# A long two-block network on one core: the experts' second chunk of weights waits in SBUF and is copied into place, and the out-projection of the recurrence begins inside its last pair

## What is computed

```python
def moe_swiglu(xn, w_router, w_gate, w_up, w_down):
    ...
    for e in range(N_EXPERTS):
        y = y + combine[:, e:e + 1] * swiglu(xt, w_gate[e], w_up[e], w_down[e])

def rwkv7_mixer(h, ...):
    ...
    for d in range(2):
        ...
        o = rwkv7_scan(*ins)
        ...
        dir_out.append((group_norm(o, gn_w, gn_b) + bonus.reshape(nB, S, D)) * g.astype(F32))
    y = dir_out[0] + dir_out[1]
    return y.astype(h.dtype) @ w_o
```

## Time and profile before

| what | value |
|---|---|
| three runs | 2826.64, 2830.97, 2832.77 us |
| the profiled execution's own time | 2826.99 us |
| its span | 2825.3 us |
| PE busy | 2639.8 us (93%) |
| DVE, ACT, POOL busy | 672.7, 431.5, 87.9 us |
| HBM read | 568.37 MB, mean 203 GB/s |

### The profile page before, as it was taken

One profiled execution on the slowest core, in us unless ns is written; L12 is line 12 of the kernel. 1 busy time (PEld: TensorE's weight loads), 2 busy tenths in 40 slices (PEclk: granted clock), 3 DMA queues, 4 the chain that ended last, 5 costly groups with the idle time before them and its releaser, 6 DMA issues. The chain is left out here.

```text
span 2825.3 us, 76095 instructions
## 1 busy us (share of the span) xinstructions
PE 2639.8 (93%) x34633; PEld 2195.9 (78%) x34633; DVE 672.7 (24%) x1740; ACT 431.5 (15%) x1040; POOL 87.9 (3%) x168
## 2 busy tenths in 40 slices
PE   8899999989979999999999999899999799989998
PEld 6677777668869999989989897666667688877664
DVE  4511000181120110110110101410043577761001
ACT  1111000111110100100100101410011444441000
POOL 0100000010000000000000000000000000010000
PEclk9899999999989999999999999999999898889999
DMA  7344344543429999999999995354443000002442
GB/s 216 119 136 135 120 157 139 154 133 119 152 79 399 407 407 407 408 407 407 407 407 407 407 400 172 112 174 155 156 142 119 5 7 5 6 5 97 158 153 89
DMA packets 290525, 571.23 MB, mean 202 GB/s; under 512 B 18326, under 2 KB 181140, under 8 KB 290404
## 3 DMA queue, kind: packets, MB, share of 16 engines
q1 hardware_dynamic: 290404, 569.49, 55.8%
HBM read 568.37 MB, written 5.28 MB: 203 GB/s over the span
## 5 line engine op out<-in xcount | busy, mean ns | idle before, releaser
L1793 PE MATMUL ps<-xg,ring 128*64 128x80 f32 x14336 | 516.4, 234 | 7.7 <-issue 2.3
L1793 PEld LDWEIGHTS ps<-xg,ring 128*64 128x64 f32 x14336 | 503.5, 138 | 18.6 <-DMA ring<-in_moe_w_up_dram 9.3
L1388 PE MATMUL ps<-xT,ring 128*128 128x256 f32 x1728 | 379.8, 380 | 4.7 <-PEq L452 3.0
L1388 PEld LDWEIGHTS ps<-xT,ring 128*128 128x128 f32 x1728 | 328.8, 190 | 65.2 <-issue 22.4
L1400 PE MATMUL ps<-ring,hidden 128*128 128x512 f32 x688 | 301.8, 593 | 0.0
L1809 PE MATMUL ps<-hidden,expert_down 128*64 128x80 f32 x7168 | 260.3, 233 | 10.4 <-DVE hidden L1885 5.7
L1809 PEld LDWEIGHTS ps<-hidden,expert_down 128*64 128x64 f32 x7168 | 252.0, 137 | 16.8 <-DVE hidden L1885 7.6
L1400 PEld LDWEIGHTS ps<-ring,hidden 128*128 128x128 f32 x688 | 131.0, 190 | 147.2 <-issue 145.1
L618 PE MATMUL ps<-ring,xT 128*128 128x256 f32 (+1 forms) x1056 | 225.8, 376 | 7.2 <-PEq L1269 3.9
L618 PEld LDWEIGHTS ps<-ring,xT 128*128 128x128 f32 x1056 | 197.0, 194 | 34.6 <-issue 9.0
L618 PE MATMUL ps<-xT,ring 128*128 128x256 f32 (+1 forms) x944 | 213.3, 388 | 11.1 <-PEq L596 4.5
(11 more groups left out here) (384 smaller groups left out, 2474.7 us busy)
## 6 DMA issues: line engine op xcount, KB each, us to landing
ring<-in_moe_w_gate_dram SPq DMA_DIRECT2D x128, 896.0 KB, 16.6
ring<-in_moe_w_up_dram SPq DMA_DIRECT2D x128, 896.0 KB, 16.8
expert_down<-in_moe_w_down_dram SPq DMA_DIRECT2D x96, 1024.0 KB, 17.3
ring<-in_mlp_w_dram SPq DMA_DIRECT2D x64, 1024.0 KB, 5.4
ring<-in_w_xkv_dram SPq DMA_DIRECT2D x16, 1024.0 KB, 5.3
expert_down<-in_moe_w_down_dram SPq DMA_DIRECT2D x32, 512.0 KB, 16.5
ring<-in_ffn_w_gate_dram SPq DMA_DIRECT2D x11, 1024.0 KB, 5.5
ring<-in_ffn_w_up_dram SPq DMA_DIRECT2D x11, 1024.0 KB, 5.3
```

The source lines that it names most:

```text
L1388: mm = pe.matmul(bank[:, m * SEQ:(m + 1) * SEQ], w[:, c, m * P:(m + 1) * P], self.xT[:, c, :], start=(c == 0), stop=(c == KC - 1))
L1793: mm = pe.matmul(bank[b][o:o + HEAD, at, :], w[:, c, f * P + o:f * P + o + HEAD], xg[:, p * E_STEP + c, :], start=(p == 0 and c == 0 and a ...
```

## The change

1. **A waiting place.** A tile `second` of 56 KB per partition lives through the first block: 8 pieces of 1792 elements. The tiles named under "Places in SBUF" become parts of it, and so cost no room of their own. `expert_waiting(kind, p, n)` gives the place of a gate or up piece.
2. **The second chunk is loaded ahead.** `expert_ahead_gate` also loads both halves of chunk 1's gate weights and the first half of its up weights (a half is two pieces in one transfer, 1792 KB); `expert_ahead_up` also loads the second half of the up weights.
3. **Eleven chunks are moved into place.** For chunks 1 to 11 (`MOVED = 11`, the items 0 to 2 less the first chunk) the gate and up weights land in `second`, and are copied into their slot in `ring` when PE is done with the piece there: gate pieces by ACT, up pieces by POOL. Such a copy waits for the half's transfer and for the piece's last product, and only then may PE read the piece. SP loads the next chunk but one into the waiting place: the order becomes gate and up of chunk g + 1, then down of chunk g. ACT's and SP's loops over the first 3 items are written out; from item 3 on all is as before.
4. **The out-projection joins the recurrence's block.** Seven turned columns (`turn(0)` to `turn(6)`) are put between the links of the last pair's chain. DVE copies them to `xT` (L3101 of the new kernel). After the pair's last product PE runs `project_out`: 42 products of six sums, the turn of the last column, then the other 22 products; `turn_only` and `add_rows` go. SP loads the MLP's first weights inside this block, once the last pair's factors are made.
5. **Small:** the columns' copies in `constants` count on another semaphore; the dense feed-forward part keeps its own load semaphores.

```diff
+    def expert_waiting(self, kind, p, n):
+        at = (E_PIECES * (1 - kind) + p) * E_STEP * E_WIDE
+        return self.second[:, at:at + n * E_STEP * E_WIDE].rearrange("p (c f) -> p c f", c=n * E_STEP)
+
+    def load_expert_ahead(self, sp, kind, half, e, cols):
+        n = E_PIECES // 2
+        src = self.expert_src[kind][e, :, half * n * E_STEP:(half + 1) * n * E_STEP, cols].rearrange("a p c f -> p (a c) f")
+        sp.dma_start(self.expert_waiting(kind, n * half, n), src).then_inc(self.ahead_loaded[kind][half].sem, 16)
...
     def expert_ahead_gate(self, sp):
...
+        for half in range(2):
+            self.load_expert_ahead(sp, 0, half, slice(0, 1), second)
+        self.load_expert_ahead(sp, 1, 0, slice(0, 1), second)
...
+        def move_ready(eng, kind, done, g, p):
+            eng.wait_ge(waiting[kind][p // half_of], 16 * (g + 1))
+            eng.wait_ge(done, g * E_PIECES + p + 1)
...
+                def load_ahead(g):
+                    k = g % n
+                    for kind in range(2):
+                        for half in range(2):
+                            sp.wait_ge(moved[kind], (g - 2) * E_PIECES + half_of * (half + 1))
+                            self.load_expert_ahead(sp, kind, half, of_item[g // n], slice(k * E_WIDE, (k + 1) * E_WIDE))
...
+                for g in range(1, MOVED + 1):
+                    if g < MOVED:
+                        load_ahead(g + 1)
+                    load_down(g)
...
+            @block.gpsimd
+            def _(pool):
+                for g in range(MOVED):
+                    for p in range(E_PIECES):
+                        move_ready(pool, 1, up_done, g, p)
+                        pool.tensor_copy(self.expert_in(1, p), self.expert_waiting(1, p, 1)).then_inc(loaded[1][p], 16)
+                        pool.wait_ge(loaded[1][p], 16 * (g + 2))
+                        pool.sem_inc(moved[1], 1)
...
+                for i in range(FIRST):
+                    for g in range(i * n, (i + 1) * n):
+                        if g < MOVED:
+                            for p in range(E_PIECES - 1):
+                                move_gate(g, p)
+                        activate(g)
+                        if g < MOVED:
+                            move_gate(g, E_PIECES - 1)
+                    close(i)
...
+                def project_out():
+                    for p in range(4):
+                        pe.wait_ge(m.piece_loaded[(run.first + first_piece + p) % RING], run.value[first_piece + p])
+                    pe.wait_ge(m.evac_dve.sem, m.evac_dve.at(len(turned_banks)))
+                    wait(pe, "second_ready", LAST, 4)
+                    for c in range(LAST):
+                        for n in range(FIRST_SUMS):
+                            add_to(n, c)
+                    wait(pe, "out_ready", LAST, 2)
+                    turn(LAST)
+                    for c in range(LAST):
+                        add_to(FIRST_SUMS, c)
+                    pe.wait_ge(m.evac_dve.sem, m.evac_dve.at(VECTOR_TURNS))
+                    for n in range(FIRST_SUMS + 1):
+                        add_to(n, LAST)
+                    for c in range(KC):
+                        add_to(FIRST_SUMS + 1, c)
...
-                    mixer.chunks(work, u)
-                m.turn_only(u, m.xT, loads=lambda sp: plan.begin(sp, plan.kinds))
-            m.add_rows(m.xT, 256, u, add=False)
+                    mixer.chunks(work, u, u, lambda sp: plan.begin(sp, plan.kinds))
```

More of the change, by code:

```diff
@@ L217, in __init__ @@
         self.mlp = self.mlp_signals("ffn_")
+        self.mlp["loaded"] = [[sem(f"ffn_{kind}{p}_loaded") for p in range(2)] for kind in ("gate", "up", "down")]
         self.moe = self.mlp_signals("moe_")
@@ L243, in mlp_signals @@
         s = {n: sem(pre + n) for n in ("gate_done", "up_done", "down_done", "act_done", "hidden_ready")}
-        s["loaded"] = [[sem(f"{pre}{kind}{p}_loaded") for p in range(2)] for kind in ("gate", "up", "down")]
         return s
@@ L2335, in gates_and_keys, with chunks @@
             s.over(n)
-    def chunks(self, ctx, y):
+    def chunks(self, ctx, y, into, loads):
         m = self.m
@@ L2576, in _ @@
                     normalise(pairs - 1, d)
+                take_sums()
             @block.tensor
@@ L2750, in pair @@
                         solve_first(i, 1, d)
+                    if last:
+                        turn(6)
                     for d in range(2):
```

139 lines of the change are left out of this document (107 added, 32 removed).

## The result

The changed kernel takes **2805.06 us** (median of 4 runs, 2802.84 to 2806.51). The kernel before took 2831.34 us beside it (2826.64 to 2832.77). The ratio is 0.9912 with a 95% interval of 0.9896 to 0.9928: faster by 26.3 us. Forecast were 2802.3 us, a range of 2795 to 2815 and a gain of 26.7 us. The profiled execution took 2806.05 us, with a span of 2804.3.

What follows compares the result with a forecast made beforehand. The experts' stage ends when its bytes are in, and PE idles at the recurrence's end. Gains of 12.0 and 14.7 us make 26.7, taken from a base of 2829.0: 2802.3 us, range 2795 to 2815.

Steps and rivals of the forecast that it cites:

- The first transfer, 3.9 us later: Experts' start: the stream's first transfer waits for pieces 0 and 1 to be used and moved, going out at 848.6.
- The second half's 1.2 us: Experts' start: the second gate half waits for piece 3's copy behind table load and Silus, losing another 1.2 us.
- The second limit, 0.9 us: Experts near chunk 12: PE's own pace delays chunk 13's gate loads; 0.9 us taken off the gain.
- The extra transfers ahead, at nothing: Before the experts: 7.34 MB more loaded ahead in two idle transfer stretches, charged at no cost.
- POOL's copy, 1.6 to 3.2 us: Experts: estimated time for POOL to copy one up piece of 1792 elements into its slot.
- The threshold of 2.7 us: Experts' start: POOL copies up to 2.7 us cost nothing; at 3.5 us they cost 3 to 4 us.
- Part two, 14.7 us: Out-projection at the recurrence's end: 30.5 us against 45.17, a gain of 14.7 us, between 12.5 and 16.9.
- POOL copies of 3.5 to 5 us: Rival, experts: slow copies make the second up half late, 17.7 us gained in all, some 2811 us; chance 0.07.
- POOL holds up DVE: Rival, experts: POOL copies delay DVE's products into hidden, PE loses 2.1 us a chunk, no change at 2831; chance 0.05.
- POOL sets the pace: Rival, experts: 44 up copies in a row make the kernel slower, from 7.0 us a copy; chance 0.04.
- The last pair does not yield: Rival, out-projection: lower PE clock and turns delaying the chain leave a gain of 7.7 us, 2809 us; chance 0.04.
- part one: Experts: loading chunk 1's gate and up weights ahead gains 12.0 us, between 8 and 14.1.

Runs made afterwards that it cites:

- experiment 12: Rerun of experiment 9 (the changed kernel with chunk 2's up halves ahead of down of chunk 1, then gate, down, up): 2796.93 us.
- experiment 4: Changed kernel with SP's order turned to gate of chunk g + 1, down of g, up of g + 1: 2799.95 us.
- Experiment 3: Changed kernel with a fourth item written out and moved through the waiting place (FIRST = 4): 2804.39 us.
- experiment 9: Experiment 4's order, except that chunk 2's gate and up halves both go out ahead of down of chunk 1: 2800.95 us.
- experiment 6: Changed kernel with the last pair's seven turns placed behind its chain instead of inside it: 2805.55 us.
- experiment 1: Changed kernel with the out-projection put back as before, so the experts' part alone: 2819.95 us.
- experiment 5: Changed kernel with every up piece copied twice by POOL: 2809.37 us.
- experiment 7: Experiment 4 with chunk 2's weights loaded piece by piece and ACT's fourth gate copy of chunk 0 ahead of its table load and Silus: 2803.4 us.
- experiment 8: Experiment 7 with four items written out and moved (FIRST = 4): 2802.95 us.
- experiment 10: Experiment 9 with experiment 7's start, the first chunk ahead loaded piece by piece: 2798.03 us.
- experiment 11: Experiment 4's kernel run once more: 2800.61 us.

## Why the prediction was right, and which of its steps were not

**What bounds the kernel: right.** The stage ends when its bytes are in. The arithmetic of bytes, corrected by what the windows show, gives the two gains that it was worked out for within 0.7 us: 8.6 for 9.3 in the change; and in experiment 12, 330 GB/s over the first 60 us are 11.4 us of standing transfers, before it was 336 over 40 us, 7.0, and nothing stands later: 18.05 - 4.4 = 13.7 for 849.8 - 836.1 = 13.7.

**The first transfer, 3.9 us later: right.** It went out 7.8 us into the stage, against 3.8 before. **The second half's 1.2 us: right in itself, but not net.** From 10 to 20 us into the stage the transfers had 364 GB/s, 1.1 us short of full; but the kernel before had 374 there and 401 and 397 in the next 20 us, together 1.2 us short as well, which the forecast did not count. Together the two steps were charged 5.1 us, and the windows show 3.6. ACT's copies took 1.70 us (1.71 forecast from the earlier trace rows). So the net after the start is 14.4 us, not 12.9.

**The second limit, 0.9 us: the step that failed.** It measured 5.8 us. The mechanism was named rightly: chunk 13's gate weights may load only when PE has used chunk 12's first piece, and PE comes late there. But how late was mis-sized. The forecast let PE lose 3 us once, to chunk 7's last down piece, and start chunk 12 near 1156, 315 us into the stage. It started 317.8 us into it, and where the down pieces come in time it starts at 310.5 (experiment 4, 1151.84 - 841.30). PE lost 1.01 and 0.20 us at chunk 6, 2.88 at chunk 7, 0.32 and 0.29 at chunk 10, all to down pieces; and after the wait of 2.88 us chunk 7's down phase took 9.54 us instead of 7.92, in a window with a clock of 0.83. Of the 0.9 us, too, no sum is given: 1160.8 less 1159.6 is 1.2. The sentence that failed reads "On SP the down pieces stand behind the next chunk's halves; at 27 us a chunk they still land in the order in which PE wants them". The order is right and the time is not: PE can be ahead of the stream by what has landed and is wanted next, and the pieces wanted next were the last on the queue. Experiment 3 shows that this is a pace and no single loss, experiments 4, 9 and 12 that it goes when the order is turned. Since 1.5 us too much was charged at the start, and the byte arithmetic falls 0.7 us short, the sum missed by only 2.7 us: 12.0 + 1.5 - 4.9 + 0.7 = 9.3.

**The extra transfers ahead, at nothing: nearly right.** They found idle transfer time, as forecast, but SP's issuing held the cross-attention's block open for 0.5 us more.

**POOL's copy, 1.6 to 3.2 us: right**, 1.68 us, near the low end, where the nearest row (the MEMSET of the earlier trace rows) had put it. The estimate from the Trainium skill (GPSIMD Engine Reference, Elementwise: side-by-side cycle accounting), 1.54 us, is 0.14 us too low, and by either the sum stays. The threshold of 2.7 us holds as far as one run above it, at 3.5 us, can tell.

**Part two, 14.7 us: right, 1.4 too low.** The turns lengthened the chain by 0.6 us and not 1.3, the 64 products took 28.1 (18.40 + 9.66) and not 28.5; the rest is the last turn and the ends of the rows. The 1.3 us were close to what the turns cost, 1.2 or more; what the forecast did not have is that the chain's clock would rise with them (experiment 6). And the 45.17 us that it set out from hold 1.7 us of a low clock at the products, which another execution did not have (experiment 1); without them part two gains 14.3. DVE was ready nearly 9 us early, as forecast (8 to spare).

**The rivals.** POOL copies of 3.5 to 5 us: fell, 1.68. *POOL holds up DVE*: fell. The products into `hidden` kept their 488 and 404 ns and PE's chunk its 23.26 us (872.36 to 895.62), and so it was in experiment 5, where POOL copied for twice as long. The Trainium skill (SBUF: State Buffer, Who interferes with whom) has DVE take the shared ports only in its two-port modes or with two inputs from SBUF, and the trace agrees. *POOL sets the pace*: fell, by the same rows. *The last pair does not yield*: fell; the products ran at 18.40 us for 42, 0.438 each, with no slower stretch.

**The base.** 2829.0, between the profiled execution and the median, was a fair one: the kernel before had medians of 2828.06 to 2831.34 in the batches here. 2831.34 - 26.3 and 2829.0 - 26.7 differ by the base more than by the gain. That the gain came out within 0.4 us is luck in part: part one's 2.7 us too much and part two's 1.4 too little work against each other, and so do the 1.5 and 4.9 us inside part one.

## What to carry to other kernels

When weights are loaded ahead into a waiting place, look at the whole queue: the lead that counts is that of the piece wanted next, and a transfer of the present chunk that stands behind the next chunk's holds the engine to the stream's pace whatever lies ready beyond it. Account for a stage whose end is set by bytes with windows aligned to its start; the missing GB/s, in us at the full rate, gave the two gains worked out here within 0.7 us. And before you start a transfer earlier, see what stands behind it: where the next one waits for the compute engine, much or all of the earlier start is spent there (experiments 7 and 8 gained nothing by it, experiment 10 half). Where small products fill the gaps of a chain, look at the clock of both versions before you call the gaps slack.

## What was not expected of the hardware

A wait of PE can cost more than its length, but need not. After 2.88 us of idle time the next 224 records took 9.54 us in place of 7.92, with a clock of 0.83 in the 10 us around it, a mean of its two levels, 2.4 and 1.2 GHz. The same came after waits of 2.87 or 2.88 us in experiment 1 (9.61) and twice in experiment 3 (9.41 and 9.61). In experiment 5 it did not:

```profile
1041.58 4.92 PE L1852 MATMUL ps<-hidden,expert_down 128*64 128x80 f32 x128 [2.87 <-DMA expert_down<-in_moe_w_down_dram]
```

The other 96 records behind this one took 3.54 us, all at the full pace, and so it was after 2.63 us in experiment 6 and 3.17 in experiment 8. The waits of 1.01 us at chunk 6 and 0.32 at chunk 10 cost nothing more either (4.91 and 4.92 us for 128 records). And in experiment 6 chunk 12 met a low clock with no idle time above 0.5 us in the 35 us ahead of it. So no length of a wait that decides it can be read from these runs.

Short products can run at half the clock although PE is recorded as busy: the last pair's chain did so for about 3 us in all three kernels without turns in it, and in none of the eleven with them.

One execution is a sample of the clock. The same kernel reached the experts 3.4 us apart in two executions (experiments 4 and 11), with the stage 836.9 us both times; in experiments 9 and 12 the granted clock of 5 us at the stage's start, 1.00 or 0.66, went with 1.4 us of the whole stage; and the same 64 products took 29.55 or 27.87 us. A comparison of two profiles within 2 us needs a look at the clock first.
